# A two-block transformer kernel: its first weights and tokens loaded in pieces, 21 turns of the identity at its start, attention scores issued in pairs, and the turn of the meta tokens moved

## The reference, cut to what matters

```
first_block, layer l = 0, 1:
  hn = rmsnorm(h, norm_mix[l])
  l == 0: diff_attention(hn): q, k, v = hn @ W; 16 heads of 64 in 8 pairs;
          softmax(q1 k1 - slope*|distance|) - lambda * softmax(q2 k2 - ...), times v; norm of each head; @ Wo
  l == 1: neighborhood_attention(hn): 16 heads, bias from a table near the token, softmax, times v; @ Wo
  h += mix;  h += swiglu(rmsnorm(h), gate, up, down)      # 2816 wide
  h += sigmoid(rmsnorm(h) @ ple_gate) * (p[l] @ ple_proj)
second_block: 16 meta tokens are put ahead of the 256; forgetting attention (8 heads) beside a convolution;
  @ w_out;  h += relu(rmsnorm(h) @ w1)^2 @ w2             # 4096 wide
  rms_norm, and the meta tokens dropped
```

## Time and profile before

| | us |
|---|---|
| median of 3 runs | 1014.9 (1014.52 to 1014.96) |
| profiled execution, its own time | 1015.26 |
| span of the profile | 1013.4 |
| PE busy | 993.4 (98%) |
| PEld busy | 865.7 (85%) |
| DVE busy | 635.6 (63%) |
| ACT busy | 506.4 (50%) |
| POOL busy | 129.3 (13%) |

### The profile page before, as it was taken

The page is one execution under the profiler, slowest core; times in us unless marked ns, Lnnn a source line. Parts: engine busy times, 40 slices in busy tenths (PEclk is TensorE's granted clock), DMA queues, the critical chain, the costliest instruction groups (busy, mean ns, idle before and its releaser), DMA issues.

```text
span 1013.4 us, 14604 instructions
## 1 busy us (share of the span) xinstructions
PE 993.4 (98%) x5869; PEld 865.7 (85%) x5869; DVE 635.6 (63%) x981; ACT 506.4 (50%) x751; POOL 129.3 (13%) x207
## 2 busy tenths in 40 slices
PE   7999999999999999999999999999999999999997
PEld 6889788888888898988888888888989889999995
DVE  6867677555556875555765555568665877555554
ACT  7666745444444655554544444456564355434442
POOL 5000796800000000000000000012500000000000
PEclk9999999999999999999999999999999999999999
DMA  9944469955555564243475555545643337656521
GB/s 277 299 136 143 104 154 209 301 175 199 179 195 177 176 204 145 111 126 125 150 244 178 195 181 193 183 132 195 191 163 110 100 125 253 204 168 205 171 81 42
DMA packets 112724, 174.77 MB, mean 172 GB/s; under 512 B 5977, under 2 KB 73569, under 8 KB 112657
## 3 DMA queue, kind: packets, MB, share of 16 engines
q1 hardware_dynamic: 106224, 165.43, 51.0%
q0 software_dynamic: 6272, 8.15, 3.3%
q10 hardware_dynamic: 160, 0.27, 0.1%
HBM read 172.77 MB, written 1.05 MB: 172 GB/s over the span
## 4 chain that ended last, share of the span: by engine, by line
PE 91%; DVE 5%; ACT 2%; DMA 1%; issue 1%; SPq 0%; DVEq 0%; ACTq 0%
PE bank L1017 27%; PE bank L1019 27%; PE bank L1018 27%; PE bank L1130 2%; DVE wl L1531 1%; PE bank L1160 1%; PE bank L1032 1%; PE bank L1187 1%; DMA raw<-in_da_w_qkv_dram 1%; PE bank L1246 1%; PE bank L1193 1%; PE bank L1180 1%; PE bank L1140 1%; ACT wh L607 1%; PE bank L1163 0%
## 5 line engine op out<-in xcount | busy, mean ns | idle before, releaser
L1531 DVE TENSOR_TENSOR wl<-raw,wh 128x2048 fp32r<-128x2048 f32 x154 | 355.2, 2312 | 185.2 <-ACT wh L607 185.1
L607 ACT ACTIVATE wh<-raw 128x2048 fp32r<-128x2048 f32 x154 | 292.0, 1909 | 118.4 <-PE bank L1019 111.8
L1017 PE MATMUL bank<-wh,xh 128*128 128x512 f32 (+2 forms) x664 | 250.5, 377 | 1.6 <-DVE xl L1608 1.0
L1019 PE MATMUL bank<-wh,xl 128*128 128x512 f32 (+2 forms) x664 | 245.9, 370 | 0.0
L1018 PE MATMUL bank<-wl,xh 128*128 128x512 f32 (+2 forms) x664 | 245.8, 370 | 0.0
L1017 PE MATMUL bank<-xh,wh 128*128 128x256 f32 (+1 forms) x672 | 194.7, 290 | 1.0 <-DVE wl L1847 0.5
L1018 PE MATMUL bank<-xl,wh 128*128 128x256 f32 (+1 forms) x672 | 190.4, 283 | 0.0
L1019 PE MATMUL bank<-xh,wl 128*128 128x256 f32 (+1 forms) x672 | 190.4, 283 | 0.0
L1017 PEld LDWEIGHTS bank<-wh,xh 128*128 128x128 f32 (+1 forms) x664 | 125.2, 189 | 22.6 <-issue 2.0
L1019 PEld LDWEIGHTS bank<-wh,xl 128*128 128x128 f32 (+1 forms) x664 | 125.0, 188 | 22.2
L1018 PEld LDWEIGHTS bank<-wl,xh 128*128 128x128 f32 (+1 forms) x664 | 125.3, 189 | 20.3
(11 more groups left out here) (248 smaller groups left out, 854.4 us busy)
## 6 DMA issues: line engine op xcount, KB each, us to landing
raw<-in_w_ff_dram SPq DMA_DIRECT2D x32, 1024.0 KB, 5.2
raw<-in_ffn_w_gate_dram SPq DMA_DIRECT2D x44, 512.0 KB, 4.0
raw<-in_ffn_w_up_dram SPq DMA_DIRECT2D x44, 512.0 KB, 5.0
raw<-in_ffn_w_down_dram SPq DMA_DIRECT2D x22, 1024.0 KB, 5.0
raw<-in_na_w_qkv_dram SPq DMA_DIRECT2D x12, 1024.0 KB, 5.2
raw<-in_w_in_dram SPq DMA_DIRECT2D x12, 1024.0 KB, 5.2
raw<-in_da_w_qkv_dram SPq DMA_DIRECT2D x11, 1024.0 KB, 11.5
raw<-in_ple_w_gate_dram SPq DMA_DIRECT2D x8, 1024.0 KB, 5.0
```

The lines of the kernel that those rows point to most:

```text
L607: nc.scalar.activation(wh[:, i % RING, :], raw[:, i % RAW, :], ACT.Copy).then_inc(s_hi, 1)
L1017: nc.tensor.matmul(dst, lh, rh, start=start, stop=False, skip_group_check=True)
L1019: return nc.tensor.matmul(dst, ll, rh, start=False, stop=stop, skip_group_check=True)
L1531: nc.vector.tensor_tensor(wl[:, i % RING, :], raw[:, i % RAW, :], wh[:, i % RING, :].bitcast(F32), ALU.subtract).then_inc(s_lo, 1)
```

## The change

The change has seven parts.

1. x is loaded as two halves of columns (both token blocks of columns 0 to 511, then of 512 to 1023). Units 0 to 3 are loaded in four pieces of 256 KB, each with its own semaphore, and the second half of x is issued between units 0 and 1. Both split engines go piece by piece (128x512) through units 0 to 3, and the first eight feature blocks of x are made 256 columns wide instead of 128.
2. TensorE turns the identity 13 times before the gains and 8 times behind the first turns of x (`WARM`). The second eight turns of x stand inside `first_pair`, behind the third block of unit 0.
3. `quarter("k", 0)` stands ahead of `spread_root`, and takes unit 2 piece by piece.
4. The meta tokens' norm and turn leave the start and go to slot 9 on all three engines; step 8 in slot 10 waits for them. Their buffers move.
5. Scores come in pairs: an even step issues scores s and s+1, into separate columns of the banks, and waits for `shifted` s-1; an odd step issues none. `shift(s)` of an even s waits for score s+1.
6. The tail of layer 0: VectorE's `mix(13)` goes ahead of `shift(14)`, and its first low half ahead of `shift(15)`. ScalarE's split of unit 15 goes ahead of `copy_turned(14)`.
7. The tail of layer 1: the first high half (ScalarE) goes ahead of exponentials 14, the first low half (VectorE) ahead of `shift(15)`; VectorE's `values_out(1, 2)` goes behind `shift(15)`.

```diff
@@ SyncE
+            def load_x(c):
+                cols = slice(512 * c, 512 * c + 512)
+                for b in range(TB):
+                    sp.dma_start(h[:, b, cols], ...[:, b, cols]).then_inc(s_x[c], 16)
+            load_x(0)
...
+                if i < PIECED:
+                    n = dst.shape[1] // 4
                     for k in range(4):
+                        sp.dma_start(dst[:, n * k:n * k + n, :], ...).then_inc(s_piece[i][k], 16)
+                        if (i, k) == (0, 3):
+                            load_x(1)
@@ TensorE
+            def first_turns(c):
+                pe.wait_ge(s_x[c], 32)
+                for k in range(4):
+                    for b in range(TB):
+                        ins = nc.tensor.transpose(first_bank(c, k)[:, b * P:(b + 1) * P],
+                                                  h[:, b, (4 * c + k) * P:(4 * c + k + 1) * P], ident[:, :])
+                    ins.then_inc(first_turned.sem, 1)
...
+                        if (kh, k) == (0, 2):
+                            first_turns(1)
...
-                        if s >= 1:
+                        if s >= 2 and b == 0:
                             wait(pe, shifted, l, s - 1)
...
-                            ins = nc.tensor.matmul(bank[4 + m][:, 0:256], q_t[...], ...
+                            ins = nc.tensor.matmul(bank[4 + m][:, S * b:S * b + S], q_t[...], ...
...
             def attention_step(l, s):
-                score(l, s)
+                if s % 2 == 0:
+                    score(l, s)
+                    score(l, s + 1)
                 apply(l, s)
...
+            for _ in range(WARM[0]):
+                nc.tensor.transpose(bank[0][:, 0:P], ident[:, :], ident[:, :])
...
+                    first_turns(0)
+                    for _ in range(WARM[1]):
+                        nc.tensor.transpose(bank[0][:, 0:P], ident[:, :], ident[:, :])
+                    pe.wait_ge(s_gcols, 1)
...
+                keys = quarter("k", 0)
+                if l == 0:
+                    run(keys)
                 spread_root(mix, bank[4])
-                run(quarter("k", 0))
-
-                if l == 0:
-                    meta_turn()
+                run(keys)
...
+                    if l == 0 and slot == META_SLOT + 1:
+                        need("meta", 0, 0)
                     for s in STEPS[slot]:
                         attention_step(l, s)
+                    if l == 0 and slot == META_SLOT:
+                        wait(pe, p_copied, 0, 5)
+                        meta_turn()
@@ VectorE
-                    wait(dve, scored, l, s)
+                    wait(dve, scored, l, s + 1 if l < 2 and b == 0 else s)
...
             def tail_1():
                 shift(1, 14)
+                turn_lo("att1", 0, 0)
+                shift(1, 15)
                 values_out(1, 2)
-                shift(1, 15)
-                turn_lo("att1", 0, 0)
...
                     for s in steps:
                         attention_step(l, s)
+                    if l == 0 and slot == META_SLOT:
+                        meta_norm()
...
                     split_to(first[part, l, c] + 4)
```

More of the change, by code:

```diff
@@ L26 @@
 LAYERS = 2
+PIECED = 4
 FFN = 2816
@@ L237, in two_blocks_kernel @@
         for l in range(3):
-            TURNS += [(f"mix{l}", *k) for k in CB] + ([("meta", 0, 0)] if l == 0 else [])
+            TURNS += [(f"mix{l}", *k) for k in CB] if l else [("meta", 0, 0)]
             TURNS += [(f"att{l}", b, c) for c in range(2) for b in range(2)]
@@ L1027, in turn @@
             def turn(name, b, c):
-                if c == 1 and name != "mix0" and not name.startswith("att"):
+                if c == 1 and not name.startswith("att"):
                     need(name, b, 0)
@@ L1092, in first_pair @@
                     for k in range(4):
[L1093 to L1097, removed]
+                        wait(pe, first_lo, kh, k)
                         pe.wait_ge(s_lo, 4 * kh + k + 1)
@@ L1706, in tail_0 @@
             def tail_0():
+                mix(13)
                 shift(0, 14)
-                mix(13)
+                turn_lo("att0", 0, 0)
                 shift(0, 15)
-                turn_lo("att0", 0, 0)
                 mix(14)
@@ L1850, in _ @@
             dve.wait_ge(s_gcols, 1)
-            wait(dve, first_hi, 3, 0)
+            for c in range(2):
+                for k in range(4):
+                    gained_lo(c, k)
+                    split_block(c, k)
             for k in range(4):
-                gained_lo(0, 0, k).then_inc(first_lo.sem, 1)
+                split_block(2, k)
+            diagonal("mix0", row_roots("mix0", EPS))
             for k in range(4):
-                wait(dve, first_hi, k if k < 2 else 3, 1)
-                gained_lo(1, 0, k).then_inc(first_lo.sem, 1)
-                split_block(0, k)
-            for b in range(TB):
-                first_turn_lo(b, 1)
-            for k in range(4):
-                split_block(1, k)
-            split[0] = 2
-            split_to(3)
-            diagonal("mix0", row_roots("mix0", EPS))
-            split_to(4)
+                split_block(3, k)
+            split[0] = PIECED
             def distances():
@@ L1940, in _ @@
                     q_over_rms(0)
-                    meta_norm()
-                    wait(dve, normed, "meta", 0, 0)
                     k_out(0)
@@ L1974, in _ @@
                         {"q": q_over_rms, "k": k_out, "v": v_out}[part](c)
+                    if l == 0 and slot == META_SLOT:
+                        wait(dve, turned_hi, "meta", 0, 0)
+                        nc.vector.tensor_tensor(xl[:, :, X0 - META:X0], bank[6][:, 0:P].rearrange("p (k s) -> p k s", k=KD),
+                                                xh[:, :, X0 - META:X0].bitcast(F32), ALU.subtract).then_inc(turned_lo.sem, 1)
                 if l == 0:
```

159 lines of the change are left out of this document (65 added, 94 removed).

## The result

The changed kernel takes 1019.1 us (median of 5 runs, 1018.21 to 1021.52), the kernel before beside it 1014.96 (1014.52 to 1015.57): a ratio of 1.0043, 95% interval 1.0029 to 1.0058. It is slower by 4.1 us. Its profiled execution took 1018.85 us with a span of 1016.7; before, 1015.26 with 1013.4. The two traces are thus 3.3 us apart in span, and this is what can be read step by step.

The account below looks back on a forecast made before the run. TensorE's own stream was taken to bound the kernel (busy 993.4 of 1013.4 us). Layer 0 +0.1, clock +1.5, layer 1's pairs -2.45, its tail +1.5 and +0.75 made +1.4: 1014.9 to 1016.3 us, range 1014.0 to 1018.0.

Parts of the forecast that it names:

- the +1.4 of the sum: Whole kernel: all terms together make it 1.4 us slower, 1014.9 to 1016.3 us.
- First product at 7.0: Start: TensorE's first product moves from 8.99 us to about 7.0.
- Score 2 at 42.7, released by `shift(1)`: Layer 0's start: TensorE stalls 3.3 us for `shift(1)`; score 2 stands at 42.7, 4.0 us ahead.
- Turns of step 3 at 49.7, a lead of 1.56: Layer 0's start: TensorE stalls 2.4 us for `mix(1)`, goes on at 49.7 instead of 51.26, keeping 1.56.
- The fall of the clock behind score 2, charged 0: Stalls around steps 2 and 3: low clock mostly fills the second stall, charged 0 (0 to 1.5 us).
- Pairs at 0.35: Both layers: each pair of scores saves 0.35 us (0.15 to 0.5); layer 1's seven pairs give -2.45.
- The pieces charged nothing: Loads at the start: 256 KB pieces cost nothing, between 0 and 1 us.
- The meta stall 3.6, and 1.5 for the clock behind it: Slot 9: TensorE waits 3.6 us (2.8 to 4.2) for `meta_norm`; low clock behind it costs 1.5 (0.9 to 2.6).
- The tail of layer 0, -0.8: Layer 0's tail: 2.1 us of stalls go, last pair saves 0.35, new waits 0.8 and 0.9; net -0.8.
- The tail of layer 1, +1.5 and half a fall, +0.75: Layer 1's tail: 2.1 us stall for `values_out(1, 2)` costs 1.5 (0.5 to 2); half a 1.5 clock fall adds 0.75.
- The first rival: Clock falls behind each long stall, steps 2 and 3 included: +0.75 and +1.5 give 1018.5 us; chance 0.20.
- the third rival: Pairs save only their exit, 0.15 us each, so 13 x 0.20 is missing: 1018.9 us; chance 0.11.

Follow-up runs that it names:

- kernel 1: The changed kernel with VectorE's meta norm made behind the low half of unit 4 instead of in slot 9; 1014.09 us, ratio 0.9978.
- experiment 2: The changed kernel with `values_out(1, 2)` put back right behind `shift(14)` in layer 1's tail; 1016.93 us, ratio 1.0014.
- experiment 3: The changed kernel with 22, 30 and 16 turns of the identity filling its three TensorE stalls (score 2, meta turn, layer 1's tail); 1017.07 us, ratio 1.0013.
- kernel 4: The changed kernel without the 13 and 8 turns of the identity at the start; 1019.03 us, ratio 1.0037.
- kernel 6: The changed kernel with both the meta norm behind unit 4's split and `values_out(1, 2)` right behind shift 14; 1010.96 us, ratio 0.9954.
- Experiment 10: kernel 7 with unit 7's low half on VectorE also left until behind `shift(2)` and `mix(1)`; 1006.93 us, ratio 0.9913.
- kernel 7: kernel 6 with VectorE making shift 0 and 1 ahead of unit 6's low half; 1009.49 us, ratio 0.9942.
- kernel 8: kernel 6 with 22 turns of the identity put ahead of score 2; 1010.41 us, ratio 0.9958.
- kernel 9: The kernel before with the scores in pairs and the changed order of layer 0's tail, start and layer 1's tail as before; 1009.49 us, ratio 0.9944.
- kernel 5: The kernel before with the scores in pairs and nothing else of the change; 1011.21 us, ratio 0.9962.
- kernel 12: kernel 9 (old start) with VectorE's order of the first steps from Experiment 10; 1008.72 us, ratio 0.9934.

## Why the prediction was wrong

The forecast was 1016.3, the median is 1019.1. Two steps failed. The lead of 1.56 us at the turns of step 3 was set by a wait that I took for the last and that was not, and layer 1's tail was charged half a fall of the clock that came in full. Each is worth about 0.9 us. The balance of 3.3 us in the traces against the +1.4 of the sum, by its steps:

- **First product at 7.0**: 7.41. **Score 2 at 42.7, released by `shift(1)`**: 43.13, by `shift`. Right, though the stall was 2.8 and not 3.3, as TensorE was there at 40.3 and not at 39. (The terms of the forecast end at 38.8, which makes a lead of 8.0 and a stall of 3.9 and not 7.5 and 3.3; nothing hung on it, since `shift` set the end of the stall.) That `shift` waits for what ScalarE makes of unit 6. In the changed kernel ScalarE began on it at 37.35 us and the score was at 43.13; in kernels 1, 2 and 3 at 38.26, 38.94 and 38.63, with the score at 44.02, 44.71 and 44.40: each time 5.8 later. (In kernels 4 and 6, where ScalarE began at 37.01 and 36.07, it was 6.5 and 6.0: there VectorE was not yet free.)
- **Turns of step 3 at 49.7, a lead of 1.56**: this step failed. They came at 50.58 and 0.6 was left. I had taken `mix(1)` for the last to come. TensorE also waits there for ScalarE's copy of the turned step 0, which stands in ScalarE's order behind the exponentials of step 2, and these behind `shift(2)` and unit 7's low half. ScalarE and VectorE in the changed kernel (the last line is `mix(1)`):

```profile
49.08 0.51 ACT L701 ACTIVATE prob<-prob,row_neg 128x256 f32<-128x256 f32 x1 [2.06 <-DVE row_neg L1685]
50.08 0.36 ACT L718 ACTIVATE pt<-bank 128x256 f32<-128x256 f32 x1
```

```profile
46.06 2.29 DVE L1543 TENSOR_TENSOR wl<-raw,wh 128x2048 fp32r<-128x2048 f32 x1 [1.39 <-ACT wh L614]
48.27 0.42 DVE L1685 CUSTOM_DVE_ANT_0 prob<-bank,kb_reg 128x256 f32<-128x256 f32 x1
...
49.60 0.48 DVE L1703 SCALAR_TENSOR_TENSOR prob<-prob,row_inv 128x256 f32<-128x256 f32 x1
```

  ScalarE was idle for 2.06 us with that copy behind it. The copy ended at 50.44 and TensorE went on at 50.58. `mix(1)` had ended at 50.08, where I had forecast 49.6: so about half of the loss is the same chain coming 0.5 later than forecast, and some 0.4 is the copy that I had not looked at. Experiment 10 took a low half out of this chain, and the wait went from 3.3 (kernel 7) to 1.1. The cost in the sum: 0.95.
- **The fall of the clock behind score 2, charged 0**: right, and shown by experiments 3, 4 and 8. The second stall covers it.
- **Pairs at 0.35**: right. Eight passes take 1.14 us, and seven pairs in layer 1 gave 2.36 where 2.45 was forecast. By the Trainium skill ("TensorEngine Tiling (Array Packing)", Key Properties) a change of tiling mode drains the engine. The traces agree in that entry and exit are paid once a pair; that it is a drain they do not show.
- **The pieces charged nothing**: right as far as the traces tell. Unit 4 was split from 28.64 us on (28.35 in the earlier trace rows), 0.3 later, which is less than the 27.7 to 30.3 that this start shows from trace to trace. The Trainium skill ("DMA: Bandwidth & Descriptors", Bandwidth) advises to batch DMAs to a megabyte or more to come near the peak; the first of the windows above, with the pieces in flight, has 383 GB/s, and the row of before with whole units 388, so the trace doesn't bear it out for queued pieces.
- **The meta stall 3.6, and 1.5 for the clock behind it**: 3.83, and 1.5 by experiments 1 and 3. Right in kind and size; it began 0.9 later, at 70.9, for the lead that was missing.
- **The tail of layer 0, -0.8**: -1.2. The two new stalls, forecast at 0.8 and 0.9, were 0.8 and 0.7.
- **The tail of layer 1, +1.5 and half a fall, +0.75**: this term was mis-sized. The stall and its delay are right, 2.17 us and 1.54 (experiment 2's 3.18 less the 1.64 of experiment 3). The fall came in full, 1.64. Experiment 4 has the same stall with no fall, so a fall there is not certain, but a single execution pays all of it or nothing. How many of the executions of the changed kernel paid it is not shown. This makes 0.9, and 0.95 with the stall's 0.04.

Together 0.95 + 0.25 (meta stall) - 0.4 (tail of layer 0) + 0.1 (pairs) + 0.95 (tail of layer 1) = 1.85, and 1.4 + 1.85 = 3.25, the 3.3 of the spans. The medians differ by 0.8 us more than the spans. 0.3 of it lies around the span (2.15 us after, 1.9 before), and the other 0.5 because the profiled execution of the changed kernel was 0.25 faster than its median and that of the kernel before 0.3 slower. What these last 0.8 consist of no trace shows.

The first rival gave a time close to what came, 1018.5. Its mechanism was only half there: the falls behind the stalls of slot 9 and layer 1 did cost 3.1, and the one at step 2, on which it laid 1.5, cost nothing. What it had of that too much, the late and partly missed chain ahead of step 3 made up for: that its time came near is luck. The same holds for the third rival's 1018.9, as the pairs did save their 0.35.

One thing I did not weigh: the start was costed as TensorE's gain, and its loss in slot 9 as a price of the same change. The experiments show them apart. The pairs alone would have been a gain of 4.0, layer 0's tail one of 1.7. What the change added beside these was worth about 10 us in the wrong direction (1019.1 against kernel 9's 1009.49), of which two orders on VectorE (experiments 1 and 2, together 8.1) are nearly all.

## What to carry to other kernels

When TensorE gains a lead, write down for the next wait every engine's queue up to the instruction that releases it, all semaphores of that wait and not the one that came last before; the lead is worth what the latest of them leaves. A short result that another engine needs (a shift, a norm, a copy) belongs ahead of a long operation whose result is needed a slot later: moving two low halves of 2.3 us behind `shift` gave 4.0 us by the medians of kernels 6 and 10 (2.5 between their traces), more than the new start did. Behind the old start the same move gave 0.8: it is worth something where the waiting engine has a lead to keep. Charge a fall of the clock after a stall only where nothing else waits behind it: of the three, two cost 1.5 and 1.6 us, and the third lay inside the next stall.

## What the runs showed of the hardware

How long TensorE stood still did not tell whether the clock would fall. It fell behind stalls of 1.84 to 1.85 us (before, kernels 5 and 12, ahead of the meta turn), 1.50 (kernel 6, step 2), 2.17 (layer 1's tail, the changed kernel and kernel 1), 2.8 and 3.8 (the changed kernel, step 2 and meta turn). It stayed at 1.00 behind 1.82 at the same meta turn (kernel 9), behind 1.51 at step 2 and the same 2.17 (kernel 4), and behind 3.26 in kernel 7, ahead of step 3:

```profile
48.94 0.41 PE L1166 MATMUL bank<-ident,prob 128*128 128x128 f32 x2 [3.26 <-ACT pt L718]
```

```profile
49.00:52.00 3.00, 3.00 (x26) 3.00 (x27) 2.93 (x9) 2.85 (x6) 0.00 (x0) 1.00 1.08 341
```

Nor did it always fall at once. Behind the stall that ended at 455.61 us it was at 1.00 until 457.2; in kernel 4 it fell at 73.3, inside the stall of 3.8 us that ended at 75.04. With turns of the identity in a stall it stayed at 1.00 in all four places where they were put (kernels 3 and 8). Of these only the stall of 3.8 us at the meta turn was followed by a fall in every trace without them (the changed kernel, kernels 2 and 4).

How often it falls also differs between executions of one kernel, and makes a good part of the scatter. Of kernel 1's ten executions the four with a mean granted clock of 0.995 to 0.997 took 1011.8 to 1013.6 us, the six with 0.993 or 0.994 took 1013.8 to 1015.3.
